# Eight heads of dilated attention in one PSUM bank per token tile, and one weight slab's load moved behind the queries and keys

## The reference, cut to what matters

```python
def _dilated_attention(q, k, v):
    ...
    outs = [_dilated_branch(qh, kh, vh, w, d) for (w, d) in DILATED_BRANCHES]
    m_all = jnp.maximum(jnp.maximum(outs[0][0], outs[1][0]), outs[2][0])
    num = sum(jnp.exp(m - m_all)[..., None] * acc for (m, l, acc) in outs)
    den = sum(jnp.exp(m - m_all) * l for (m, l, acc) in outs)
    o = num / den[..., None]
    return o.reshape(B, S, D_ATTN).astype(q.dtype)
...
        attn = _rms_norm(_dilated_attention(q, k, v), attn_out_gain[i])
        rw = _rwkv7(...)
        mixed = jnp.concatenate([attn, rw], axis=-1) @ w_out[i]
```

## Time and profile before

| | us |
|---|---|
| median of 3 executions | 1494.68 |
| lowest and highest of them | 1486.62, 1497.68 |
| profiled execution, its own time | 1484.69 |
| span in its trace | 1482.9 |
| PE busy in the span | 1386.3 |
| dilated attention beside RWKV pairs 2 and 3 | about 256 to 367 of the span |

### The profile page before, as it was taken

How to read it: one execution, slowest core, us unless ns; L and a number is a source line. 1 busy time by engine, 2 the same in 40 slices (tenths; PEclk the granted TensorE clock), 3 DMA queues, 4 the chain that set the end, 5 groups by cost and what they waited for, 6 DMA issues and landing times.

```text
span 1482.9 us, 19845 instructions
## 1 busy us (share of the span) xinstructions
PE 1386.3 (93%) x7954; PEld 1115.1 (75%) x7954; DVE 742.4 (50%) x1176; ACT 620.5 (42%) x966; POOL 473.2 (32%) x172
## 2 busy tenths in 40 slices
PE   6998989787989999999998999998999997899996
PEld 5786868675778888888877888777888876766763
DVE  3267376654265523425133597445255164566665
ACT  4453354455353423223134234744435453256552
POOL 2441132000426655646424464521244610200002
PEclk9999999795999999999998999999999998899999
DMA  6221111300434445454443333121332605789964
GB/s 222 86 93 52 57 57 43 138 1 1 170 100 146 152 131 167 128 152 147 132 138 114 87 127 112 59 65 50 114 111 89 231 1 234 276 343 419 419 252 185
DMA packets 98815, 207.62 MB, mean 140 GB/s; under 512 B 6784, under 2 KB 56320, under 8 KB 92064
## 3 DMA queue, kind: packets, MB, share of 16 engines
q1 hardware_dynamic: 91808, 181.13, 35.4%
q10 hardware_dynamic: 4608, 16.78, 2.8%
q0 software_dynamic: 2304, 8.39, 1.5%
HBM read 170.63 MB, written 35.65 MB: 139 GB/s over the span
## 4 chain that ended last, share of the span: by engine, by line
PE 82%; DVE 7%; ACT 4%; issue 3%; DMA 3%; POOL 1%; SPq 0%; POOLq 0%; DVEq 0%; ACTq 0%
PE bank L526 21%; PE bank L508 13%; PE bank L510 13%; PE bank L509 13%; PE bank L2977 4%; PE bank L846 3%; PE bank L822 2%; PE bank L837 1%; PE bank L742 1%; PE bank L2924 1%; PE bank L1254 1%; PE bank L1231 1%; PE bank L2915 1%; ACT whi L437 1%; POOL wlo L445 1%
## 5 line engine op out<-in xcount | busy, mean ns | idle before, releaser
L445 POOL TENSOR_TENSOR wlo<-raw,whi 128x2048 fp32r<-128x2048 f32 (+2 forms) x83 | 378.9, 4565 | 594.8 <-ACT whi L437 567.9
L437 ACT ACTIVATE whi<-raw 128x2048 fp32r<-128x2048 f32 (+1 forms) x84 | 159.1, 1894 | 255.8 <-PE bank L510 234.1
L2110 DVE TENSOR_TENSOR ffn_relu<-ffn_relu 128x512 f32<-128x512 f32 x32 | 97.7, 3052 | 101.4 <-ACT ffn_relu L2090 101.4
L526 PE MATMUL bank<-alo,whi 128*128 128x512 f32 x352 | 139.9, 397 | 1.5 <-DVE alo L765 1.5
L526 PE MATMUL bank<-ahi,whi 128*128 128x512 f32 x352 | 137.9, 392 | 0.0
L508 PE MATMUL bank<-alo,whi 128*128 128x512 f32 (+1 forms) x344 | 136.1, 396 | 0.0
L510 PE MATMUL bank<-ahi,wlo 128*128 128x512 f32 (+1 forms) x344 | 134.1, 390 | 0.0
L509 PE MATMUL bank<-ahi,whi 128*128 128x512 f32 (+1 forms) x344 | 133.9, 389 | 0.0
L526 PE MATMUL bank<-ahi,wlo 128*128 128x512 f32 x352 | 87.8, 391 | 0.0
L526 PEld LDWEIGHTS bank<-alo,whi 128*128 128x128 f32 x352 | 66.6, 189 | 18.0 <-DVE alo L765 1.9
L526 PEld LDWEIGHTS bank<-ahi,whi 128*128 128x128 f32 x352 | 66.7, 189 | 14.1 <-issue 0.5
(11 more groups left out here) (530 smaller groups left out, 2981.7 us busy)
## 6 DMA issues: line engine op xcount, KB each, us to landing
raw<-in_w_in_dram SPq DMA_DIRECT2D x18, 1024.0 KB, 5.3
expert_gate_up<-in_expert_w_gate_dram SPq DMA_DIRECT2D x17, 1024.0 KB, 10.3
expert_gate_up<-in_expert_w_up_dram SPq DMA_DIRECT2D x17, 1024.0 KB, 13.4
expert_down<-in_expert_w_down_dram SPq DMA_DIRECT2D x17, 1024.0 KB, 7.4
raw<-in_w_ffn_up_dram SPq DMA_DIRECT2D x16, 1024.0 KB, 6.1
raw<-in_w_ffn_down_dram SPq DMA_DIRECT2D x16, 1024.0 KB, 5.6
raw<-in_w_in_first_dram SPq DMA_DIRECT2D x12, 1024.0 KB, 5.4
expert_rows_dram<-zero_rows SPq DMA_DIRECT2D x23, 512.0 KB, 6.9
```

Of the source, the lines that this page charges most:

```text
L437: nc.scalar.activation(whi[:, n % SPLIT, 0:k * c], raw[:, n % RAW, 0:k * c], ACT.Copy).then_inc(hi_made, 1)
L445: nc.gpsimd.tensor_tensor(wlo[:, n % SPLIT, 0:k * c], raw[:, n % RAW, 0:k * c], whi[:, n % SPLIT, 0:k * c].bitcast(F32), ALU.subtract).the ...
L526: ins = nc.tensor.matmul(acc, of, by, start=first and i == 0, stop=last and i == products - 1)
L2110: nc.vector.tensor_tensor(relu2[:, n % 2, :], relu[:, n % 2, :], relu[:, n % 2, :], ALU.mult).then_inc(up_sq, 1)
```

## The change

`attn_units`, `pe_attn`, `dve_attn` and `act_attn` get a mode `grouped`, which only the dilated attention uses. The eight heads of a tile write their values side by side, 64 columns each, into one bank, which is held from the first head to the last. DVE no longer divides after each head but once per tile, with one reciprocal of eight sums and one product of 512 columns, in which the eight factors are broadcast. ACT no longer waits for item i-3's product before it writes `probs_t`. `heads_out` now counts tiles here and items elsewhere, so the places that wait for it count with new numbers. And `out.0.1` is loaded with `out.1.0` behind queries, keys and values.

```diff
@@ -786,15 +786,19 @@
...
         attn_count = [0]
-
-        def attn_units(name, heads, keys, by_tile=False, lag=1, together=1, last_first=False):
+        heads_count = [0]
+
+        def attn_units(name, heads, keys, by_tile=False, lag=1, together=1, last_first=False, grouped=False):
 
...
             base = attn_count[0]
-            attns[name] = dict(items=items, base=base, lag=lag, together=together)
+            group = heads if grouped else 1
+            out = heads_count[0]
+            attns[name] = dict(items=items, base=base, lag=lag, together=together, group=group, out=out)
             attn_count[0] += len(items)
+            heads_count[0] += len(items) // group
             for i in range(len(items) + 2 * lag):
...
@@ -802,8 +806,11 @@
...
                     banks.plan(f"{name}/t{i - lag}", (probs_turned, n - lag + 1))
-                if i >= 2 * lag:
-                    banks.plan(f"{name}/o{i - 2 * lag}", (heads_out, n - 2 * lag + 1))
+                j = i - 2 * lag
+                if j >= 0 and j % group == 0:
+                    banks.plan(f"{name}/o{j // group}", (heads_out, out + j // group + 1), hold=grouped)
+                if j >= 0 and grouped and j % group == group - 1:
+                    banks.release(f"{name}/o{j // group}")
                 yield
...
@@ -824,7 +831,7 @@
...
         def pe_attn(pe, name, factors, v, probs, probs_t):
-            items, base, lag = (attns[name][n] for n in ("items", "base", "lag"))
+            items, base, lag, group = (attns[name][n] for n in ("items", "base", "lag", "group"))
             for i in range(len(items) + 2 * lag):
...
@@ -840,16 +847,19 @@
...
                     pe.wait_ge(probs_turned, base + j + 1)
-                    acc = banks.open(pe, f"{name}/o{j}")
+                    if j % group == 0:
+                        out = banks.open(pe, f"{name}/o{j // group}")
                     n = v(h, 0).shape[1]
+                    at = j % group * n
                     for b in range(keys // P):
-                        ins = nc.tensor.matmul(acc[:, 0:n], probs_t[j % (lag + 1)][:, b * P:(b + 1) * P], v(h, b),
+                        ins = nc.tensor.matmul(out[:, at:at + n], probs_t[j % (lag + 1)][:, b * P:(b + 1) * P], v(h, b),
                                                start=b == 0, stop=b == keys // P - 1)
-                    banks.filled(ins, f"{name}/o{j}")
+                    if j % group == group - 1:
+                        banks.filled(ins, f"{name}/o{j // group}")
                 yield
...
         def dve_attn(dve, steps, name, scale, band, masked, peaks, sums, heads):
-            items, base, lag = (attns[name][n] for n in ("items", "base", "lag"))
+            items, base, lag, group = (attns[name][n] for n in ("items", "base", "lag", "group"))
             for i in range(len(items) + 2 * lag):
...
@@ -867,7 +877,15 @@
...
                 j = i - 2 * lag
-                if j >= 0:
+                if j >= 0 and group > 1 and j % group == group - 1:
+                    _, t, _ = items[j]
+                    acc = banks.take(dve, f"{name}/o{j // group}")
+                    over = peaks[:, 32 + j + 1 - group:32 + j + 1]
+                    steps.link(nc.vector.reciprocal(over, sums[:, j + 1 - group:j + 1]))
+                    by_head = lambda a: a.rearrange("p (h n) -> p h n", h=group)
+                    nc.vector.tensor_tensor(by_head(heads(t)), by_head(acc[:, :]), over.unsqueeze(2).broadcast_to([P, group, H // group]),
+                                            ALU.mult).then_inc(heads_out, 1)
+                elif j >= 0 and group == 1:
                     h, t, keys = items[j]
...
@@ -890,7 +908,7 @@
...
                     acc = banks.take(act, f"{name}/t{j}")
-                    if j >= lag + 1:
+                    if j >= lag + 1 and attns[name]["group"] == 1:
                         banks.take(act, f"{name}/o{j - lag - 1}")
...
@@ -1050,7 +1068,7 @@
...
             yield from deep_units(["v0", "v1"], "v", lambda t: (qkv_out, 9 + t))
-            yield from rounds(ATTN_STEPS, attn_units("dil", NHEAD, lambda t: (t + 1) * P, by_tile=True, lag=2, together=2, last_first=True),
+            yield from rounds(ATTN_STEPS, attn_units("dil", NHEAD, lambda t: (t + 1) * P, by_tile=True, lag=2, together=2, last_first=True, grouped=True),
                               turn_dil_units(), out_dil_units())
...
@@ -1155,7 +1173,7 @@
...
         def heads1_ready(eng, t):
-            eng.wait_ge(heads_out, attns["dil"]["base"] + NHEAD * (t + 1))
+            eng.wait_ge(heads_out, attns["dil"]["out"] + NHEAD // attns["dil"]["group"] * (t + 1))
 
...
@@ -1634,7 +1652,7 @@
...
             yield from rounds(ATTN_STEPS, dve_split_dil(dve), dve_attn(dve, steps, "dil", HD ** -0.5, const("band_dilated"), masked1, peaks1,
-                                                                       esum1, lambda h, t: heads1[:, t, half(h)]), dve_norm_dil(dve))
+                                                                       esum1, lambda t: heads1[:, t, :]), dve_norm_dil(dve))
 
...
@@ -1900,7 +1918,6 @@
...
             load_gain(sp, "attn_out_gain")
-            load_slabs(sp, sp_slab, slab_no["v1"] + 1 + RAW)
             sp.wait_ge(*banks.full_at(f"v/{NT - 1}"))
...
```

More of the change, by code:

```diff
@@ L2340, in fox_heads_ready @@
         def fox_heads_ready(eng, t):
-            eng.wait_ge(heads_out, attns["fox"]["base"] + len(attns["fox"]["items"]))
+            eng.wait_ge(heads_out, attns["fox"]["out"] + len(attns["fox"]["items"]))
         def act_phase3(act):
@@ L2614, in cross_heads_ready @@
         def cross_heads_ready(eng, t):
-            eng.wait_ge(heads_out, attns["xa"]["base"] + XH * (t + 1))
+            eng.wait_ge(heads_out, attns["xa"]["out"] + XH // attns["xa"]["group"] * (t + 1))
         def sp_phase4(sp):
@@ L3410, in sp_phase5 @@
             sp.dma_start(router_b[:, NG:NG + NE], w["router_expert_b_2"][0:1, :].broadcast_to([P, NE])).then_inc(router_in, 16)
-            sp.wait_ge(heads_out, attns["xa"]["base"] + XH * NT)
+            sp.wait_ge(heads_out, attns["xa"]["out"] + XH // attns["xa"]["group"] * NT)
             sp_gate_up(sp, 1, 1)
```

## The result

The changed kernel takes 1476.48 us (median of 9 runs, 1474.13 to 1480.46). Beside it the kernel before took 1487.82 (median of 9, 1485.17 to 1497.68; the three runs shown ahead of the prediction are among these). The ratio is 0.9913, with an interval of 0.9896 to 0.9931, so it is faster by 0.9%. The predicted 1487.5 is 11 us too high, and the range began at 1478. Against the profiled executions the picture is another: 1484.69 before and 1476.87 after, 7.8 us less, where the sum was 7.2 and its result 1477.5. So the terms must be looked at, but the larger error is in the level that they were set against.

The account below looks back on a forecast made before the run. PE bounds the kernel, standing in latency waits in the dilated attention. 2.6 + 2.4 - 0.5 - 0.35 + 0.8 + 1.6 + 0.7 = 7.25, say 7.2 us, off the median 1494.68: 1487.5, range 1478 to 1496.

Parts of the forecast that it names:

- the level: Whole kernel: the 7.2 us saving was set against the three-run median 1494.68 (1487.5), not the profiled 1484.69 (1477.5).
- Rival C: Attention from 307 to 332 us: new PE wait pattern keeps the clock low, some 14 us; 1501.5 us, chance 0.05.
- The sum of 7.2: Dilated attention: savings on keys' wait, PE's waits and clock, less two new waits, come to 7.25, say 7.2 us.
- The slab, 2.6: Keys' readback ahead of PE's first score: 1.05 MB at 399 GB/s no longer stand ahead, saving 2.6 us.
- the 240 of the prediction's estimate: Queries' and keys' readback: at 240 GB/s, halfway in the skill's table, 256 KB pieces would lose some 1.7 of 2.6 us.
- The waits, 2.4 + 1.6 + 0.8 - 0.5 - 0.35 = 3.95: Attention: PE's bank waits save 2.4, state 1.6, DVE's divisions 0.8; transposes cost 0.5, third tile's scores 0.35 us.
- the two new ones: PE waits: transposes after the second tile's turn for `cols_lo`, 0.5 us; scores behind the third tile for its division, 0.35 us.
- rival B: Inside the attention: ACT and DVE latency swallows the gains, only the readback's 2.6 us remain; 1492 us, chance 0.20.
- The clock, 0.7: Attention from 303 to 307 us: without the 0.99 us idle time the clock stays up, 0.7 of 1.7 us counted.
- DVE is not the bound: DVE in the attention: the 9.2 us of work it loses are off the path almost everywhere.
- Rival A: Last third of the attention: the clock comes back early, at say 348 us; 4 us more, 1483.5 us, chance 0.20.

Follow-up runs that it names:

- all three edits: The changed kernel with PE's waits for score readings, DVE's wait for every head's product and DVE's old division work given back together: 1485.88 us, ratio 0.9982.

## Why the prediction was wrong

**The level failed.** The step is "I set the same saving against the median: 1487.5". The profiled execution had the short dip, and is the fastest of before that was seen; two of the three runs shown, 1497.68 and 1494.68, were of the upper group. The 10 us between profile and median were no unexplained offset that stays under any change: two later traces of before are 7.6 us longer, some 6 us of it by the long form of the dip behind the 0.99 us wait, and that wait is one that the change removes. None of the 9 runs of the changed kernel is above 1481. The slab moved alone leaves that wait and yet shows no long dip in 12 executions, so which of the two parts spares it in the changed kernel is open. The own forecast of 1477.5, which the text gives as the sum against the profile, did not even lie in the range, though the range should have held the results by both anchors.

**Rival C had the mechanism and the wrong kernel.** It prices the low clock from 307 to 332 us at 14 us, as a danger of the change, at 0.05. The low clock from 307 to 321 was a cost of before: in two traces, and by their times in 31 of 81 executions.

**The sum of 7.2 came near the 7.8 partly by luck.** In the two profiled executions PE's work ahead of the attention ended 1.0 us later in the changed kernel, so the sum has 8.8 us to explain up to the end of the span, and 8.7 up to the rows at 359.81 and 352.19. These 8.7 fall in three parts. The wait for the keys gives 3.3. PE's idle time from the first score to those rows goes from 12.64 to 9.89 us, which is 2.75. PE's busy time in the same stretch goes from 80.35 to 77.71 us for the same products, which is 2.64.

- **The slab, 2.6: mis-sized by 0.7 in the pair.** Over all traces it is about 3 us. The argument of the Trainium skill (DMA: Bandwidth & Descriptors, "Rules for kernel authors") for large transfers was set aside by one window at 399 GB/s. It was a window of 256 KB pieces, as the prediction reads it: the slab had landed 7.0 us behind its issue at 256.09. But the pieces do not run at that rate from their start. They ran at 350 and 326 GB/s in the changed kernel, and at 229 and 250 from 262 to 264 us in the kernel with the slab moved alone, which is where the 240 of the prediction's estimate lies.
- **The waits, 2.4 + 1.6 + 0.8 - 0.5 - 0.35 = 3.95: right in kind, 1.2 too high in sum.** All waits named are gone, and the two new ones are there: 0.84 (bound 0.9), and 1.11 where 1.0 was worked out. What the sum left out is that PE then meets ACT's lateness: 0.85 at 307.58, 0.55 at 325.95, 0.71 at 349.99, and 3.70 where 3.32 was. That is rival B in part: the transposes wait 6.7 us for ACT from 255 to 372 us, where they waited 5.0.
- **The clock, 0.7: mis-sized, by 1.0 at least.** The clock stays at 1.00 from 303 to 307, so the whole 1.7 comes off. It is the larger part of the 2.64; the rest is not broken down. Over executions of before the dip is worth that plus some 7 us in 4 of 10.

Given back one at a time, the banks, the state and DVE cost 3.4, 1.3 and 1.1 us by medians, none of it clear of the intervals. Together they cost 9.4, with their part of the clock. "DVE is not the bound" is true, and yet with its divisions back PE's waits for it were longer.

**What is left.** From the lower group the change brings 10.5 us by medians, 3 more than the sum. 2.3 of that is again the level: the profiled execution of before lies that far below the median of its group, while the one of the changed kernel lies 0.4 above its own. PE's work ahead of the attention, which the change doesn't touch, ended at 260.3 us in that execution and at 262.1 and 261.8 in the two later ones, so up to 1.8 us of the level is scatter there. Rival A is no part of the profiled pair; it stands in four traces of kernels with the grouping and briefly in one without, and three of the changed kernel's nine runs have a mean clock of 0.973 or 0.974 where the profiled one has 0.971. That it lowers the median is not shown. Nor is it shown why moving the slab alone spares before its long dip.

## What to carry to other kernels

When the median of the runs and the profiled execution differ by more than the term you work out, the difference is the first thing to explain: look at the mean granted clock of each run, and price every short wait of PE that has a low clock behind it at the longest dip that it can have, not at the one in your trace. Where waits stand on one another's engines, give them back together before you believe their sum. And a wait that "the change leaves" is worth the same look: ACT's table loads, moved into its own idle time, gave as much again (11 us) as the whole change.

## What the runs showed of the hardware

A wait of PE of about 1 us can bring the clock down to its lower level (1.2 of 2.4 GHz) and need not, and its length does not tell. 0.99 us did so in three traces of before, and did not in two kernels, that with PE's waits given back and that with all three edits. 1.12, 1.25 (at 320.55 in before) and 1.54 us did not; 1.19, 1.58 and 1.70 us did. How long it stays low varied between executions of one program: from 303 us it was low to 307, to 321 and to 324. In the long case PE was busy for 14.00 of 14.00 us, by the profile, at 0.50. The Trainium skill (TensorE: Matmul & The Clock Gate, "What's actually happening") has activity releasing the throttle; here full activity in the profile's sense did not for that long, while half of it were products of 64x64 weights (L1360).

An exchange of ACT's function tables cost 1.28 us, and the next instruction began 0.02 us behind it.

Queued transfers of 256 KB moved at 399 GB/s in before, where they stood behind a transfer of 1 MB, and at 229 to 350 GB/s from 261 to 264 us in two kernels where nothing stood ahead of them (the changed one and that with the slab moved alone).
